# First block's attention: dilated scores of two heads issued together, both maxima in one step, weight splits moved to later steps

## What is computed

```
def dilated_attention(q, k, v):          # 12 heads: 3 groups g x 4 slots
    # group g with (w, d): query t attends to t, t-d, ..., t-w
    for g, (w, d) in enumerate(DIL_PAIRS):       # (128,1) (512,4) (2048,16)
        o, lse = banded_attention(strided(q), strided(k), strided(v), w // d)
    alpha = softmax(lses over the groups)
    o = sum(alpha * outs)
ob, _ = banded_attention(qb, kb, vb, SWA_WINDOW - 1, sinks)   # 8 heads on 2 k/v heads
mix = sigmoid(ga) * (oa @ w_branch_a) + sigmoid(gb) * (ob @ w_branch_b)
```

## Time and profile before

| | us |
|---|---|
| median of three runs | 1316.66 (1315.03 to 1316.85) |
| the profiled execution, its own time | 1314.84 |
| its span, first to last instruction | 1313.0 |
| TensorE busy | 1303.2 (99%) |
| TensorE weight loads busy | 1102.6 (84%) |
| VectorE busy | 925.0 (70%) |
| ScalarE busy | 641.0 (49%) |
| GpSimd busy | 67.4 (5%) |

### The profile page before, as it was taken

The page is one execution under the profiler, slowest core; times in us unless marked ns, Lnnn a source line. Parts: engine busy times, 40 slices in busy tenths (PEclk is TensorE's granted clock), DMA queues, the critical chain, the costliest instruction groups (busy, mean ns, idle before and its releaser), DMA issues.

```text
span 1313.0 us, 17226 instructions
## 1 busy us (share of the span) xinstructions
PE 1303.2 (99%) x6977; PEld 1102.6 (84%) x6977; DVE 925.0 (70%) x1190; ACT 641.0 (49%) x839; POOL 67.4 (5%) x145
## 2 busy tenths in 40 slices
PE   9999999999999999999999999999999999999997
PEld 7887788888888888887888888888888878888886
DVE  5798767766547666788876666776666888676665
ACT  7777645343344444357554444444443576543441
POOL 3121000000000000000300000000000003000000
PEclk9999999999999999999999999999999999999999
DMA  9643466555555555553565555565555444755550
GB/s 297 207 154 106 122 239 193 193 192 192 191 198 190 192 192 193 192 150 108 183 205 191 192 192 193 166 236 190 188 188 187 161 129 131 241 188 190 188 185 33
DMA packets 155311, 238.11 MB, mean 181 GB/s; under 512 B 4264, under 2 KB 110784, under 8 KB 155232
## 3 DMA queue, kind: packets, MB, share of 16 engines
q1 hardware_dynamic: 154576, 235.95, 54.8%
q0 software_dynamic: 384, 0.54, 0.3%
q10 hardware_dynamic: 272, 0.52, 0.1%
HBM read 235.95 MB, written 1.05 MB: 180 GB/s over the span
## 4 chain that ended last, share of the span: by engine, by line
issue 86%; PE 9%; POOL 2%; POOLq 1%; DVE 1%; ACT 1%; DVEq 0%; DMA 0%; SPq 0%
PE ps L1603 2%; PE ps L1604 2%; PE ps L1605 2%; POOL drs L574 1%; POOLq L573 1%; PE ps L1673 1%; POOL lrs L574 1%; PE ps L1756 0%; DMA xres<-in_x_dram 0%; PE ps L1765 0%; ACT ebuf L754 0%; PE ps L1780 0%; PE ps L1734 0%; DVEq L1094 0%; DVE ebuf L1112 0%
## 5 line engine op out<-in xcount | busy, mean ns | idle before, releaser
L543 DVE TENSOR_TENSOR wlo<-raw,whi 128x2048 fp32r<-128x2048 f32 x172 | 391.8, 2287 | 129.3 <-ACT whi L535 129.1
L535 ACT ACTIVATE whi<-raw 128x2048 fp32r<-128x2048 f32 x197 | 369.7, 1905 | 22.9 <-DMA raw<-in_w_up_dram 11.3
L1977 PE MATMUL ps<-xt_both,whi 128*128 128x512 f32 x1504 | 358.7, 390 | 0.0
L1977 PEld LDWEIGHTS ps<-xt_both,whi 128*128 128x128 f32 x1504 | 279.1, 188 | 55.9
L1982 PEld LDWEIGHTS ps<-xt_both,wlo 128*128 128x128 f32 x1504 | 193.4, 191 | 7.6
L1271 DVE TENSOR_REDUCE hid_a<-ps 128x512 f32<-128x1024 f32 (+1 forms) x98 | 115.3, 1177 | 119.0 <-PE ps L1982 119.0
L1982 PE MATMUL ps<-xt_both,wlo 128*128 128x256 f32 x1504 | 195.7, 283 | 0.0
L1603 PE MATMUL ps<-whi,ht_hi 128*128 128x512 f32 x480 | 187.7, 391 | 0.0
L1604 PE MATMUL ps<-wlo,ht_hi 128*128 128x512 f32 x480 | 187.3, 390 | 0.0
L1605 PE MATMUL ps<-whi,ht_lo 128*128 128x512 f32 x480 | 186.8, 389 | 0.0
L899 ACT ACTIVATE hid_b<-hid_a 128x512 f32<-128x512 f32 x40 | 25.2, 630 | 236.5 <-DVE hid_a L1271 236.5
(11 more groups left out here) (232 smaller groups left out, 1333.9 us busy)
## 6 DMA issues: line engine op xcount, KB each, us to landing
raw<-in_ffn_w_in_dram SPq DMA_DIRECT2D x80, 1024.0 KB
raw<-in_ffn_w_out_dram SPq DMA_DIRECT2D x44, 1024.0 KB
raw<-in_w_in_dram SPq DMA_DIRECT2D x36, 1024.0 KB
raw<-in_w_up_dram SPq DMA_DIRECT2D x16, 1024.0 KB
raw<-in_w_down_dram SPq DMA_DIRECT2D x16, 1024.0 KB
raw<-in_w_out_dram SPq DMA_DIRECT2D x8, 1024.0 KB
raw<-in_ffn_w_in_dram SPq DMA_DIRECT2D x16, 512.0 KB
raw<-in_w_out_dram SPq DMA_DIRECT2D x8, 512.0 KB
```

The source lines that it names most:

```text
L535: act.activation(whi[j][:, :], raw[j][:, :], ACT.Copy).then_inc(hi_done, 1)
L543: dve.tensor_tensor(wlo[j][:, :], raw[j][:, :], whi[j][:, :].bitcast(F32), ALU.subtract).then_inc(lo_done, 1)
L1977: pe.matmul(o(k).rearrange("p (j n) -> p j n", j=2), whi[w][:, block(b, k)], xt_both[:, :, b, :], start=b == 0, stop=False)
```

## The change

The scores of the units 2j and 2j+1 are issued together in the even step by `dilated_scores`: six products, in an order in which neighbours lie in different row halves and in different PSUM banks. Unit 3 gets PSUM space in banks 6 and 7, the units 1, 5 and 7 lie shifted in banks 2 and 3 with another order of the groups (`DIL_ORDERS`), which needs two more mask rows. Units 6 and 7 do not both fit: one product of unit 7 goes with unit 6, the other two stay in step 7 (`DIL_LATE`). VectorE takes both maxima in the even step, with the probabilities of the unit before between them. The first `pair_outputs` gets a wait for four maxima. In `STEP_LO` the halves of unit 17 move from the steps 1, 2 to 4, 5, those of 18 from 4, 5 to 7, 8, those of 19 from 6, 6 to 9, 10, those of 20 from 9, 11 to 11, 13.

```diff
--- before.py
+++ after.py
...
 STEP_HI = {0: 17, 2: 18, 5: 19, 7: 20, 11: 21, 13: 22, 16: 23}
-STEP_LO = {1: ((17, 0),), 2: ((17, 1),), 4: ((18, 0),), 5: ((18, 1),), 6: ((19, 0), (19, 1)), 9: ((20, 0),),
-           11: ((20, 1),), 16: ((21, 0), (21, 1)), 17: ((22, 0), (22, 1)), 18: ((23, 0),)}
-DIL_ORDER = (0, 2, 1)
+STEP_LO = {4: ((17, 0),), 5: ((17, 1),), 7: ((18, 0),), 8: ((18, 1),), 9: ((19, 0),), 10: ((19, 1),), 11: ((20, 0),),
+           13: ((20, 1),), 16: ((21, 0), (21, 1)), 17: ((22, 0), (22, 1)), 18: ((23, 0),)}
+DIL_ORDERS, DIL_LATE = ((0, 2, 1), (1, 0, 2)), 7
 SQUARES_3, NORM_2, SUMS_3, NORM_3, TURN_QB = 0, 0, 1, 3, 5
...
-        mask = little("mask", [P, 6, TOK], BF16)
+        mask = little("mask", [P, 8, TOK], BF16)
         ident = little("ident", [P, P])
...
             pool.wait_ge(mask_mod, 1)
-            for kind in range(5):
+            for kind in range(7):
                 pool.affine_select(out=mask[:, kind, P:TOK], in_=mask[:, kind, P:TOK], compare_op=ALU.is_ge,
                                    fill=NEG, base=0, pattern=[[-1, P]], channel_multiplier=1)
-            for kind, least in ((0, 0), (5, 0), (3, 1)):
+            for kind, least in ((0, 0), (3, 0), (7, 0), (5, 1)):
                 pool.affine_select(out=mask[:, kind, 0:P], in_=mask[:, kind, 0:P], compare_op=ALU.is_ge,
...
         scores1 = ps[:, 2:4, :].rearrange("p b n -> p (b n)")
+        def dilated_place(u):
+            r, n = u % 2, P * (unit1(u)[1] + 1)
+            first = r * (TOK - n)
+            if u == 3:
+                return ps[:, 6:8, :].rearrange("p b (g n) -> p (b g) n", n=TOK)[:, 1:1 + DIL_G, :]
+            return scores1.rearrange("p (g n) -> p g n", n=TOK)[:, r:r + DIL_G, first:first + n]
...
                 dve.wait_ge(pt_ready, u - 2)
-            dve.wait_ge(s_ready, u + 1 if u < HALF else u - u % 2 + 2)
+            dve.wait_ge(s_ready, DIL_LATE if u == DIL_LATE - 1 else u - u % 2 + 2)
             i, e, s = u % 4, ebuf1[u % 3], scores1
                 w = width_of(u)
-                n = w // DIL_G
+                n, kinds = w // DIL_G, slice(2 * (u % 2), 2 * (u % 2) + DIL_G)
                 dve.tensor_tensor_reduce(e[:, 0:w].rearrange("p (g n) -> p g n", g=DIL_G),
-                                         s[:, 0:DIL_G * TOK].rearrange("p (g n) -> p g n", g=DIL_G)[:, :, 0:n],
-                                         mask[:, 0:DIL_G, TOK - n:TOK], SCALE, -3e38, ALU.add, ALU.max, top[:, i, 0:1])
+                                         dilated_place(u), mask[:, kinds, TOK - n:TOK], SCALE, -3e38, ALU.add, ALU.max, top[:, i, 0:1])
                 dve.drain()
...
                 c = r * BW + u % 2 * TOK
-                dve.tensor_tensor_reduce(e[:, r * w:(r + 1) * w], s[:, c:c + w], mask[:, 3, TOK - w:TOK],
+                dve.tensor_tensor_reduce(e[:, r * w:(r + 1) * w], s[:, c:c + w], mask[:, 5, TOK - w:TOK],
                                          SCALE, -3e38, ALU.add, ALU.max, top[:, i, r:r + 1])
...
                 for r in range(KV):
-                    dve.tensor_tensor_reduce(e[:, r, 0:TOK], s[:, r, :], mask[:, 4 + t, :],
+                    dve.tensor_tensor_reduce(e[:, r, 0:TOK], s[:, r, :], mask[:, 6 + t, :],
                                              1.0, -3e38, ALU.add, ALU.max, top[:, i, r:r + 1])
...
             dve.drain()
-            for b in range(2):
+            for b, kind in ((0, 2), (1, 1), (1, 4)):
                 for j in range(2):
-                    m = dve.tensor_scalar(mask[:, 2 - b, j * P:(j + 1) * P], dist4[:, b, :], 0.0, NEG,
+                    m = dve.tensor_scalar(mask[:, kind, j * P:(j + 1) * P], dist4[:, b, :], 0.0, NEG,
                                           ALU.not_equal, ALU.mult)
...
                 if i < HALF:
-                    maxima(dve, i)
+                    if i % 2 == 0 or i == DIL_LATE:
+                        maxima(dve, i)
                     if i >= 1:
                         probs(dve, i - 1)
+                    if i % 2 == 0 and i + 1 != DIL_LATE:
+                        maxima(dve, i + 1)
                 elif i < UNITS and i % 2 == 0:
...
+        def dilated_scores(pe, u):
+            v, qt = u - u % 2, unit1(u)[1]
+            if u == 0:
+                pe.wait_ge(qk_out, 6)
+            else:
+                pe.wait_ge(top_ready, u)
+            if v + 1 != DIL_LATE:
+                parts = ((v, 0), (v, 1), (v + 1, 1), (v + 1, 0), (v, 2), (v + 1, 2))
+            elif u == v:
+                parts = ((v, 0), (v, 1), (v, 2), (v + 1, 2))
+            else:
+                parts = ((v + 1, 1), (v + 1, 0))
+            for w, g in parts:
+                h, n = unit1(w)[0], P * (qt + 1)
+                r = h % 2 ^ (g == 1)
+                rows, i = slice(r * HD, (r + 1) * HD), DIL_ORDERS[w % 2].index(g)
+                m = pe.matmul(dilated_place(w)[:, i, :], qkt1[rows, 2 * g + h // 2, qt * P:(qt + 1) * P],
+                              qkt1[rows, 6 + 2 * g + h // 2, 0:n], start=True, stop=True)
+            m.then_inc(s_ready, 1 if v + 1 == DIL_LATE else 2)
         def scores(pe, u):
-            if u in (0, HALF):
-                pe.wait_ge(qk_out, 6 if u == 0 else QK1_BANKS)
-            if u >= 1 and (u < HALF or u % 2 == 0):
+            if u == HALF:
+                pe.wait_ge(qk_out, QK1_BANKS)
+            if u % 2 == 0:
                 pe.wait_ge(top_ready, u)
-            s, (h, qt) = scores1, unit1(u)
+            h, qt = unit1(u)
             n = P * (qt + 1)
-            if u < HALF:
-                parts = [(h % 2 ^ (g == 1), 2 * g + h // 2, 6 + 2 * g + h // 2) for g in range(DIL_G)]
-            else:
-                parts = [(r, 12 + h, 16) for r in range(KV)]
-            for i, (r, qtile, ktile) in enumerate(parts):
-                rows = slice(r * HD, (r + 1) * HD)
-                c = DIL_ORDER.index(i) * TOK if u < HALF else i * BW + u % 2 * TOK
-                m = pe.matmul(s[:, c:c + n], qkt1[rows, qtile, qt * P:(qt + 1) * P], qkt1[rows, ktile, 0:n],
+            for r in range(KV):
+                rows, c = slice(r * HD, (r + 1) * HD), r * BW + u % 2 * TOK
+                m = pe.matmul(scores1[:, c:c + n], qkt1[rows, 12 + h, qt * P:(qt + 1) * P], qkt1[rows, 16, 0:n],
                               start=True, stop=True)
...
             pe.wait_ge(o_out, u)
+            if u == 0:
+                pe.wait_ge(top_ready, 4)
             nk = unit1(u)[1] + 1
                 for i, (g, k) in enumerate(terms):
-                    j = DIL_ORDER.index(g) * nk + k
                     for r in range(2):
-                        h = unit1(u + r)[0]
+                        h, j = unit1(u + r)[0], DIL_ORDERS[r].index(g) * nk + k
                         m = pe.matmul(ps[r * HD:(r + 1) * HD, 6, 0:P], proj1[:, k, V1 + (4 * g + h) * HD:V1 + (4 * g + h + 1) * HD],
...
                 if i < HALF:
-                    scores(pe, i)
+                    if i % 2 == 0 or i == DIL_LATE:
+                        dilated_scores(pe, i)
                 elif i < UNITS and i % 2 == 0:
```

## The result

The changed kernel takes 1321.03 us, median of six runs (1319.56 to 1321.5), beside 1316.05 for the kernel before on the same chip (1315.03 to 1316.85). The ratio is 1.004, with a 95% interval of 1.003 to 1.005: slower by 5.0 us. The profiled execution took 1321.5 us, its span 1319.7. Against the profiled execution of before that is 6.7 us more.

What follows compares the result with a forecast made beforehand. TensorE, busy for 99% of the span, was taken to bound the kernel. The terms -2.4 + 1.7 + 1.5 + 3.2 + 0.2 = +4.2 us, on the median 1316.66, made 1320.9 us; range 1317.6 to 1322.8.

Steps and rivals of the forecast that it cites:

- The gain: TensorE's paired scores, steps 0 to 7: 1.26 us saved in passes and 1.12 in score visits, together 2.4 us.
- Rival 4: Products of two units don't run side by side, six need four passes: +5.5 us, 1322.2; chance 0.07.
- Unit 17: Step 5: its split ends on VectorE at 110.4, piece 20 falls due at 108.7; TensorE stalls 1.7 us.
- the other gate operation should now meet the norm of step 3: GpSimd's second gate scaling slows VectorE's norm in step 3, by 0 to 0.8 us, taken as 0.6.
- The hold of the split itself: A two-block split on VectorE takes 2.21 us instead of 1.41 while GpSimd scales gates: 0.8 us.
- Rival 2: GpSimd's holds miss VectorE in steps 3 and 4: first stall only 0.3 us, total +2.8, 1319.5; chance 0.14.
- Unit 18: Third piece of step 9: split ends at 128.57 against 127.07 on TensorE, stall 1.5 us.
- Unit 19: First piece of step 11: split ends at 135.67 against 132.50 on TensorE, stall 3.2 us, the largest term.
- Unit 20's half: Second half moved to step 13, ahead of step 14's maxima: 0 to 1.2 us, taken as 0.2.
- rival 3: TensorE's clock falls to 1.2 GHz in the longest stall: 1.6 us more lost, 1322.5; chance 0.07.
- The sum: All terms together: -2.4 + 1.7 + 1.5 + 3.2 + 0.2 = +4.2 us, making 1320.9 us.
- the idle time in one TensorE slice: Sign of being right: the profile after shows TensorE's idle time in one slice near 130 us.

Runs made afterwards that it cites:

- the best version: Changed kernel with splits moved into VectorE's idle stretches, and one GpSimd gate scaling made to wait until unit 17 is split: 1312.95 us, ratio 0.9984.
- the later splits alone: Kernel before with only the change's new STEP_LO table, scores not paired: 1326.21 us, ratio 1.0076.
- the version kept busy: Changed kernel with 24 unread transposes on TensorE ahead of the wait of gate piece 36: 1320.64 us, in a second set 1319.48 us.

## Why the prediction was right

The time came out at 1321.03, forecast 1320.9, in the forecast's own way for the most part. By its steps:

- **The gain.** Forecast 2.4 us, measured 2.29 in the changed kernel and, without any wait around it, 2.20 in the best version (58.99 less 56.79). Passes and visits were priced right to a tenth. Rival 4 is refuted: six products of 256 columns took 1.50 us, three passes and the fixed 0.22, not four.
- **Unit 17.** Forecast 1.7, measured 1.56. The term "the other gate operation should now meet the norm of step 3" failed. GpSimd reached that gate operation earlier and it met the probabilities of unit 2, which lost 0.26 where I had put 0.6; the norm ran from 100.21, after that operation, so no run shows whether it would be held. The hold of the split itself, 0.8, was there. Counted from the first scores, the split ended 0.4 earlier than forecast and the piece fell due 0.2 earlier, which is why the stall hardly moved. Rival 2 is refuted: both holds took place, and with GpSimd's operation made small 1.05 us came back.
- **Unit 18.** Forecast 1.5, measured 1.63: the row's duration plus the signal.
- **Unit 19.** Forecast 3.2, measured 3.21.
- **Unit 20's half.** Forecast 0.2, measured 0.21. The size was right and the reason incomplete: it takes the half and GpSimd's hold on the last probabilities together, and without either it vanishes.
- **The clock.** This step failed. The forecast, at 0.62, had no clock term, and rival 3 had 0.07. It came true in every traced execution of the changed kernel. Its price too was wrong: 1.6 us, from "if the low level lasts as long as the 3.2 us stall". The low level began when the wait was nearly over, or after it, and lay on the work behind it, some 6 us in two executions, so 2.7 us were lost there, and 1.6 in the third. The Trainium skill, "TensorE: Matmul & The Clock Gate", section "HAM oscillation", had said that waits between stretches of matmuls can put the engine back on half its clock. By that rule the trace agrees for the wait of 3.2 us; the two of 1.6 us show no fall.
- **The sum.** Without the clock the changed kernel's distance is 4.5 us above before (63.46 less 58.99), forecast 4.2. With it, the profiled pair lies 7.2 apart in distance and 6.7 in span. The medians lie only 5.0 apart, since the unpriced clock cost less in most executions than in the profiled one (by their mean granted clock). Even so the difference was 0.8 more than forecast, and the median of before that it was added to came out 0.6 lower, at 1316.05 and not 1316.66. The two errors cancel. The direction and the waits were forecast rightly; that the total hit to 0.1 us is luck.

In "What the profile after would show", every line under "right" came true but the idle time in one TensorE slice: it is shared by two, 2.9 us in 100 to 132 us and 3.1 in 132 to 165, and lowers no digit of the page. One under "wrong" came true as well: a granted clock below full in the slice around 130 us. The two don't exclude each other, and I ought to have made the clock a term.

## What to carry to other kernels

Work that is moved away from a late place must be laid against the due time of who waits for it: the same splits put into idle stretches turned 5 us of loss into 1.4 to 2.1 of gain (two sets of runs). The wait of TensorE of 3.2 us cost up to nearly twice its length, since the clock fell on the work behind it, and the two of 1.6 us only their own length, so the longest wait is the first to be broken up. When VectorE is late by less than a microsecond, look for a GpSimd operation beside it, and let that one wait.

## What was not expected of the hardware

**The clock after a wait.** It fell around the end of a wait of 3.2 us in all five profiled executions that have one with TensorE idle: 0.6 to 1.0 us before the end in four, 1.3 us after it in one. By the granted clock of short stretches it stayed at half for 6.8 us in three of them (the changed kernel's first two, and with GpSimd's operation made small) and for 3.4 in two (the changed kernel's third, and the later splits alone). What decides between the two is open. Waits of 1.6 us, and an idle rest of 0.42 us behind 2.78 us of idle-time transposes, left it full.

**Two starts of the program.** The first scores come at 89.48 to 90.24 us in nine profiled executions, and at 91.48 to 92.19 in four, each of another kernel. The difference lies at the first matmuls. The changed kernel, early start:

```profile
5.93 0.66 PE L1646 MATMUL ps<-ident,xres 128*128 128x128 f32 x4 [0.41 <-DMA xres<-in_x_dram]
6.42 1.25 PE L2076 MATMUL ps<-ident 128*128 128x128 f32 x10
```

and the version kept busy, late start:

```profile
6.11 1.11 PE L1646 MATMUL ps<-ident,xres 128*128 128x128 f32 x4 [0.49 <-DMA xres<-in_x_dram]
7.01 2.34 PE L2079 MATMUL ps<-ident 128*128 128x128 f32 x10
```

The same transposes take nearly twice as long, while the granted clock reads 1.00 in both. What causes it isn't shown. One kernel's runs fall into two groups some 2 us apart (before: 1314.5 and 1316.7), and where such a kernel was profiled, an early start lay in the lower group and a late one in the upper (with GpSimd told to wait, 1314.36). The kernel before has no profile with a late start. It is why distances inside a trace say more here than medians.

**GpSimd holds VectorE's one-input operations too.** A scaling of the gates of about 1.1 us cost a split 0.79 us, the probabilities at L1129 0.79 and those at L1120 0.26 to 0.85. The Trainium skill, "GPSIMD Engine Reference", section "Specifications", names VectorE's 2-port mode beside instructions with two SBUF inputs. The splits read two SBUF tensors, and their hold agrees with the second half. That the probabilities, with one large SBUF input, are held would fit the first half, which I had passed over, if they run in that mode; no trace here shows the mode.
